# A two-layer block in split fp32 on one core: the order of work in the first group of matmuls, and idle products ahead of it

## What is computed

```python
def first_block(x, ...):
    h = rmsnorm(x, norm_mix_g[i])          # x * rsqrt(mean(x*x) + EPS) * g
    u = h @ w_in[i]                        # 2048 x 12288
    c_g, b_g, xa, za, q, fl, iv, og, ga, gb = jnp.split(u, split_idx, axis=-1)
    ...                                    # short convolution, gated recurrence, gates
    x = x + m @ w_o[i]
    ...
def second_block(x, ...):                  # windowed attention and retention, then a norm
```

## Time and profile before

| | |
|---|---|
| median of 3 runs | 2648.33 us |
| the profiled execution, its own time | 2646.47 us |
| its span in the trace | 2645.2 us |
| PE busy | 2614.1 us (99%) |
| DVE busy | 1263.2 us (48%) |
| ACT busy | 891.3 us (34%) |
| chain that ended last | PE 94%, DVE 2%, issue 2%, ACT 1% |
| PE idle before line 329, high by high | 12.4 us |
| PE idle before line 329, high by low | 5.5 us |

### The profile page before, as it was taken

The page is one execution under the profiler, slowest core; times in us unless marked ns, Lnnn a source line. Parts: engine busy times, 40 slices in busy tenths (PEclk is TensorE's granted clock), DMA queues, the critical chain, the costliest instruction groups (busy, mean ns, idle before and its releaser), DMA issues.

```text
span 2645.2 us, 28782 instructions
## 1 busy us (share of the span) xinstructions
PE 2614.1 (99%) x11718; PEld 2122.5 (80%) x11718; DVE 1263.2 (48%) x2013; ACT 891.3 (34%) x1236; POOL 73.8 (3%) x64
## 2 busy tenths in 40 slices
PE   8999999999999999999999999999999999999998
PEld 7888888888888888888888888688777777777888
DVE  7556634447424555655442353562243444443425
ACT  5633325333223222222232342332232333433323
POOL 0000000000000000000000111100000000000000
PEclk9999999999999999999999999999999999999999
DMA  5322233222234666666442232235322222222424
GB/s 193 100 72 77 75 96 96 84 76 72 88 96 127 216 215 211 215 208 214 142 170 97 88 104 96 72 104 163 93 59 77 80 80 72 75 77 80 167 96 152
DMA packets 159972, 309.11 MB, mean 117 GB/s; under 512 B 11040, under 2 KB 15392, under 8 KB 158816
## 3 DMA queue, kind: packets, MB, share of 16 engines
q1 hardware_dynamic: 159040, 305.70, 36.2%
q0 software_dynamic: 224, 1.15, 0.1%
q10 hardware_dynamic: 576, 0.43, 0.1%
HBM read 298.84 MB, written 8.39 MB: 116 GB/s over the span
## 4 chain that ended last, share of the span: by engine, by line
PE 94%; DVE 2%; issue 2%; ACT 1%; DMA 0%; POOL 0%; SPq 0%; DVEq 0%; ACTq 0%; POOLq 0%
PE bank L329 86%; PE bank L701 2%; PE bank L1132 1%; PE bank L1241 1%; PE bank L1215 1%; PE bank L720 1%; PE bank L1230 1%; PE bank L1121 1%; PE bank L399 0%; DVE WL L375 0%; ACT WH L354 0%; DVE SC L483 0%; DMA X<-in_xT 0%; DVE Y L1945 0%; POOL AC L1984 0%
## 5 line engine op out<-in xcount | busy, mean ns | idle before, releaser
L329 PE MATMUL bank<-XH,WH 128*128 128x512 f32 (+1 forms) x2880 | 1148.8, 399 | 12.4 <-DVE XL L475 5.7
L329 PE MATMUL bank<-XH,WL 128*128 128x512 f32 (+1 forms) x2880 | 1112.1, 386 | 5.5 <-DVE WL L375 5.5
L329 PE MATMUL bank<-XL,WH 128*128 128x512 f32 (+1 forms) x2880 | 1109.0, 385 | 0.0
L375 DVE TENSOR_TENSOR WL<-RAW,WH 128x1024 fp32r<-128x1024 f32 x443 | 544.0, 1230 | 965.6 <-ACT WH L354 964.7
L354 ACT CAST WH<-RAW 128x1024 fp32r<-128x1024 f32 x443 | 463.2, 1048 | 1179.7 <-PE bank L329 1179.6
L329 PEld LDWEIGHTS bank<-XH,WH 128*128 128x128 f32 x2880 | 542.9, 189 | 132.2 <-issue 20.7
L329 PEld LDWEIGHTS bank<-XL,WH 128*128 128x128 f32 x2880 | 543.1, 189 | 118.6 <-issue 15.1
L329 PEld LDWEIGHTS bank<-XH,WL 128*128 128x128 f32 x2880 | 542.2, 188 | 118.8 <-DVE WL L375 7.6
L329 PE MATMUL bank<-WH,XH 128*128 128x512 f32 x384 | 155.4, 405 | 0.0
L329 PE MATMUL bank<-WL,XH 128*128 128x512 f32 x384 | 149.6, 390 | 0.0
L329 PE MATMUL bank<-WH,XL 128*128 128x512 f32 x384 | 149.4, 389 | 0.0
(11 more groups left out here) (242 smaller groups left out, 1647.0 us busy)
## 6 DMA issues: line engine op xcount, KB each, us to landing
RAW<-in_w_in SPq DMA_DIRECT2D x303, 512.0 KB, 3.6
AST<-in_w_ada SPq DMA_DIRECT2D x192, 256.0 KB, 4.0
RAW<-in_w_out SPq DMA_DIRECT2D x40, 512.0 KB, 3.6
RAW<-in_w_o SPq DMA_DIRECT2D x32, 512.0 KB, 3.6
RAW<-in_w_gate SPq DMA_DIRECT2D x32, 512.0 KB, 3.6
RAW<-in_w_a SPq DMA_DIRECT2D x16, 512.0 KB, 4.2
RAW<-in_w_b SPq DMA_DIRECT2D x16, 512.0 KB, 4.3
XT<-in_xT SPq DMA_DIRECT2D x4, 1024.0 KB, 6.7
```

The source lines that it names most:

```text
L329: ins = nc.tensor.matmul(bank[b][:, cols], l, r[:, cols], start=first, stop=final)
L375: nc.vector.tensor_tensor(WL[:, m % NSPL], RAW[:, m % NRAW], WH[:, m % NSPL].bitcast(F32), ALU.subtract).then_inc(lo.sem, lo.step(m))
```

## The change

For n below 2, that is for the first four steps, exactly k+1 weight units are made at step k, on ACT and on DVE. The raw rows of x are made one step ahead of PE instead of two (`1` in the calls of `act_dense` and `dve_dense`), and `start_part` pulls them by another table, 2, 4, 6, 8, 9, 11, ... instead of 4, 6, 8, 10, .... The square of row j is made behind row j+2 instead of row j+1, with four scratch buffers instead of two, so it waits for the sum of row j-4. The norm comes ahead of the bound's constants. The product that sums the squares stands one step later on PE. And PE begins with eleven products of `ONES` by `ONES`, 128 columns each, into bank 7, which nothing reads.

```diff
 def hi_upto(n, k):
+    if n < 2:
+        return k + 1
     return min(n + AHEAD if n or k else 0, len(UNITS) - 1) + 1
 def lo_upto(n, k):
-    return min(hi_upto(n, k), n + AHEAD + k % 2 if n else 3)
+    return hi_upto(n, k) if n < 2 else min(hi_upto(n, k), n + AHEAD + k % 2)
...
+    SQ_AT = (0, 1, 3, 4)
...
-            for j in range(k - 1 if k else 16, 16 if k == 15 else k):
-                if j > 2:
-                    A.wait_ge(dve, (yield dve, ("acc0", j - 2)))
-                nc.scalar.activation(SC[:, j % 2 if j else 2], X0[:, j], ACT.Square
+            for j in range(max(k - 2, 0) if k < 11 else k - 1, 16 if k == 15 else k if k > 9 else k - 1):
+                if j > 4:
+                    A.wait_ge(dve, (yield dve, ("acc0", j - 4)))
+                nc.scalar.activation(SC[:, SQ_AT[j % 4] if j else 2], X0[:, j], ACT.Square
...
-                    nc.vector.tensor_tensor(SC[:, 2], SC[:, 2], SC[:, j % 2], ALU.add
+                    nc.vector.tensor_tensor(SC[:, 2], SC[:, 2], SC[:, SQ_AT[j % 4]], ALU.add
...
 def start_part(eng, bound, norm):
-        for n in range(7):
+        for n in range(10):
             if eng in raw_feed:
-                yield from raw_feed[eng].upto(min(16, 2 * n + 4))
-            yield
+                yield from raw_feed[eng].upto(2 * n + 2 if n < 4 else 4 + (4 * n + 1) // 3)
+            yield
+        if eng == "pe":
+            yield
+        yield from norm
+        yield
         if bound:
             yield from bound
-        yield
-        yield
-        if eng == "pe":
-            yield
-        yield from norm
-        yield
...
     def pe():
+        T.wait_ge(dve, (yield dve, "ones"))
+        for n in range(11):
+            nc.tensor.matmul(bank[7][:, 0:128], ONES[:, :], ONES[:, :], start=True, stop=True)
...
-        yield from act_dense(("fl", 0), raw_feed["act"])
+        yield from act_dense(("fl", 0), raw_feed["act"], 1)
...
-        yield from dve_dense(("fl", 0), raw_feed["dve"])
+        yield from dve_dense(("fl", 0), raw_feed["dve"], 1)
```

## The result

| | before | after |
|---|---|---|
| median of 16 runs | 2648.12 us (2644.81 to 2649.07) | 2643.65 us (2641.79 to 2644.60) |
| ratio | | 0.9984 (0.9976 to 0.9992) |
| the profiled execution, its own time | 2646.47 us | 2642.10 us |
| its span | 2645.2 us | 2640.8 us |
| first product of the heads (line 701, now 702) | 145.05 us | 142.27 us |

The median is 4.5 us lower, 0.17%; the forecast was 3.3. The heads' first product is a landmark at the end of what the change reorders: up to there 2.8 us are won. The other 1.6 us between the two profiled executions arise 1500 us later, where nothing was changed, and the experiments show that they come and go from execution to execution.

What follows compares the result with a forecast made beforehand. PE bounds the kernel, busy 99% of the span, so only its idle or slow time can be won. 1.70 + 0.26 + 2.57 - 1.2 = 3.3 us off 2648.33 gives 2645.0 us, range 2642.8 to 2647.1.

Steps and rivals of the forecast that it cites:

- signs of being wrong: What would show the forecast wrong: slow spacing beyond 6 us, a wait at the sum, or no wait at 52.
- Term 1: Kernel start: eleven products fill PE's wait for x, real matmuls start at full rate at 5.75; 1.70 us won.
- If the clock rises again some 3.6 us after the first work, at 4.7: Kernel start: eight products would run slow and three fast, ending near 5.4, before the operands are there.
- Term 2: Weights in order of need: the stalls at 13.30 and 35.55 go, winning 0.26 and 2.57 us.
- It holds by some 0.7 us: Last sum of squares ready at about 38.1, PE asks at 38.9, with unit 4 landing at 21.2.
- the load of unit 4 comes later: Rival, chance 0.07: each us past the 0.7 of slack at the sum goes to PE; about 2646.
- The four scratch buffers: First group: they take away ACT's waits for sums, but ACT is not late, so worth nothing by themselves.
- 0.26: First stall, at 13.30: PE lost 0.26 us, which goes with unit 1 cast before row 2.
- Term 3: Start of the second group: a new wait for the low part of unit 8, 1.2 us lost.
- The rest of the kernel follows PE, and shifts with it: After the reordered start: the rest only shifts, so the whole gain is 3.3 us.
- more is won at the start: Rival, chance 0.2: unprofiled executions have an extra slow stretch at the start, which the products remove; 1.7 more, 2643.3.
- PE falls to half rate at the new stall: Rival, chance 0.1: slow matmuls follow the new wait at the second group; price 1.6 us, 2646.6.

Runs made afterwards that it cites:

- second trace: The changed kernel run again unaltered, beside the kernel before on the same chip: median 2642.89 us, ratio 0.9984.
- only products: The kernel before with only the eleven products of ones added, in the old order: median 2646.73 us against 2646.72, ratio 0.9998.
- load 4 first: The changed kernel with the load of weight unit 4 issued ahead of the load of rows 11 to 15 of x: median 2642.85 us, ratio 0.9984.
- filled wait: The changed kernel with eighteen more idle products of ones in PE's 4.3 us wait near 1711: median 2641.95 us, ratio 0.9977.
- constants early: The changed kernel with the eight-column constants made at the fourth step of the first group: median 2642.71 us, ratio 0.9983.

## Why the prediction was right, and where it was off

The time lies in the range and on the side forecast, 1.35 us under the predicted value (2643.65 against 2645.0). Part of that is luck: what the change itself was to win came out 0.5 short (2.8 at the heads instead of 3.3, and 2.0 in the second trace), and the rest of the kernel, where the forecast saw nothing, gave more than the difference. Two of its own signs of being wrong came: a wait at the sum in both traces of the changed kernel, and slow spacing beyond 6 us. Its 0.2% as the least that can be told from no change was too careful, since the interval (0.9976 to 0.9992) leaves 1 out. Step by step:

- **Term 1, 1.70.** Measured 1.54. The products and their cover were right (1.06 to 5.77, not late), and both operands held. The step that was off: "If the clock rises again some 3.6 us after the first work, at 4.7". In the two traces of the changed kernel it rose near 6.2 and 7.1, so the first real matmuls were still slow. Ten traces begin with the same eleven products: in six of them PE was at full rate by the first real matmul, in two (this and only products) near 6.2, in two (the second and constants early) near 7.1. One value was carried over where there is a range.
- **Term 2, 2.83.** Both stalls went, in full. "It holds by some 0.7 us" failed: the landing of unit 4 was carried over from the old trace as 21.2, and came at about 22.3. ACT waited 4.2 us for it instead of 3, and the sum cost PE 0.33. So the rival "the load of unit 4 comes later", given 0.07, is what happened. The chain behind the landing was right: 16.92 us from the cast to the last sum, forecast 38.1 - 21.2 = 16.9. (Its terms as written add up to 16.7, and PE's 38.9 to 38.98, so that the slack would be 1.1; and two high parts take 1.34 in the earlier trace rows, not 1.24, which leaves the 0.62 as it is.) The next load now issues at 10.96, earlier than before, while unit 4 is still under way. That is not what slows it: in five other traces the next load is issued as early (10.99 to 11.66), and unit 4 lands 13.3 to 13.5 us after its issue, as before.
- **The four scratch buffers**, "worth nothing by themselves", were mispriced. Without them, and with the squares one row behind again, the chain of sums is 1.2 us longer. The step looked only at whether PE's next row was late, and not at the sum at the end of the same chain.
- **"0.26"** for the first units was right for the difference, and hid what these rules do: they are what lets PE use the full rate. Products alone won nothing, and without these rules PE waits 1.88.
- **Term 3, -1.2.** Measured -1.18, at 52.84, behind the constants. The count along the chain held to a few hundredths (50 matmuls at 0.23 and 0.87 are 12.37, not 12.35), and so did taking the constants out of it (heads 1.22 earlier).
- **"The rest of the kernel follows PE, and shifts with it"** is the step that failed by most. It shifted, and the clock behind a stall did not answer alike: one slow stretch less, 1.6 us, which another execution can have again.

Of the rivals, "more is won at the start" had the right size of extra (1.7) at the wrong place: the traces put the slow stretch that went at 1669. A longer slow start does exist, though: thirteen slow matmuls in the kernel without products, eight in the kernel before. That the number differs from run to run, as the Trainium skill's page "TensorE: Matmul & The Clock Gate", section "The HAM clock gate", says, is borne out by the changed kernel's two traces: one real matmul was slow in the first, three in the second, the last of each only in part. "PE falls to half rate at the new stall" did not happen in any of the eight traces with that stall of 0.9. The rival of unhidden weight loads fell: 22 passes took 4.71 us, 0.21 each, all at half rate.

What stays open is how the unprofiled runs divide. Before, they lie near 2645 (2 of 16), 2646.7 (4) and 2648.1 to 2649.1 (10); after, at 2641.8 to 2642.6 (6) and 2643.5 to 2644.6 (10). The steps have the size of a slow stretch, and the lowest groups are 2.8 apart, what the traces show up to the heads. The mean granted clock, which each run has to three digits, speaks for the clock as the cause: after the change it is 0.998 in all six runs of the lower group and 0.997 in all ten of the upper; the changed kernel's second set (six and five) and load 4 first (five and six) divide alike, while with the filled wait both groups read 0.998. It also speaks for stretches in mid-kernel: a slow start does not lower this figure, which reads 1.00 at 5 to 9 us in the kernel before, where the matmuls are 0.43 apart. Where in an unprofiled run its slow stretches lie is not shown. So of the 4.5 us the traces show 2.0 to 2.8 to be the change's; the remainder can be the share of executions with a slow stretch more or less, which no run here ties to the change. Why one stall of the same length is followed by half rate and another not isn't settled either.

## What to carry to other kernels

Raising the matmul clock with idle products pays only if the operands can then keep up: the products alone won nothing. Let the products run until shortly before the first real matmul: a rest of 0.62 us did no harm, while five products with 2.12 us of rest left eight slow matmuls, as many as before. Test the two edits apart and together. After a reorder, ask again for every load and every buffer of the stretch what it now holds up, with a landing time taken as a range and not as a constant. And where a microsecond is won early, look at PE's pauses of a few microseconds later on: filling the longest with idle products is cheap, and took away its slow stretch in both traces that had the products. Last, compare traces landmark by landmark before a difference in the medians is put down to an edit.

## What the runs showed of the hardware

- A stall of the same 1.8 us, in the same place of the program, was followed by half-rate matmuls in 6 of 13 traces. In two of them (before, only products) the first matmul behind it was already slow; in four the rate fell 0.6 to 1.6 us after PE was back at work at full rate (constants early: 1667.81 to 1669.30).
- The stall of 4.3 us was followed by half rate in all 11 traces without idle products in it and in neither of the two with them.
- At the start the half rate is read from the spacing alone: 0.43 us per 512 columns, as in the stretch at 1672 with a granted clock of 0.50. The profile's granted clock reads 1.00 there (before, 5 to 9 us).
- Plain fp32 products of ones of 128 columns count as work for the clock: the real matmuls are at full rate by 7.1 us or earlier in all ten traces that begin with eleven of them, and from 9.6 and 11.8 in the two that begin without. They took 0.43 us each at half rate and were 0.23 apart over 4.2 us in mid-kernel, with the real matmuls behind them at full rate.
- The load of unit 4, issued behind the same transfers, landed 13.3 to 13.5 us after its issue in seven traces and 14.1 to 14.4 in three (changed kernel twice, filled wait). Its issue itself moved from 7.7 to 8.7 us, so that it landed anywhere from 21.1 to 23.1.
